# Forgetting attention two heads at a time on halves of TensorE's array, and joint gates in the mixer

## Chip, cores and metric

One core of a Trainium2 chip runs the whole program. The metric is the device time of one execution in microseconds: three runs of the kernel before gave 2260.94 to 2266.46, median 2263.86.

## The reference, cut

A token mixer with a 16-expert layer (272 positions: 16 learned tokens and 256 inputs, width 1024) is followed by two layers of a second block (256 positions, width 1024). The change touches two places: the gates of the first mixer and the forgetting attention of the second block's first layer.

```python
def _token_mixer(h, norm_g, w_in, b_gates, ...):
    proj = jnp.einsum('bnd,dk->bnk', _rmsnorm(h, norm_g), w_in)
    rq, rk, rv, rg, mq, mk, mv, mo, gate_pre = jnp.split(proj, SPLIT_AT, axis=-1)
    ...
    gts = gate_pre.astype(f32) + b_gates.astype(f32)          # 16 columns
    log_i = gts[..., :8]                                      # 2 directions x 4 heads
    log_f = jax.nn.log_sigmoid(gts[..., 8:])
    ...
def forgetting_attention(q, k, v, log_f):                     # 8 heads of 64, 256 positions
    cum = jnp.cumsum(log_f, axis=1).transpose(0, 2, 1)
    for blk in range(seq // 128):
        lo, hi = blk * 128, (blk + 1) * 128
        s = einsum("bqhd,bkhd->bhqk", q[:, lo:hi], k[:, :hi]) * scale      # scale = 1/8
        s = s + cum[:, :, lo:hi, None] - cum[:, :, None, :hi]
        s = jnp.where(causal, s, NEG_INF)
        outs.append(einsum("bhqk,bkhd->bqhd", softmax(s), v[:, :hi]))
def fox_shortconv_mixer(h, w_in, b_f, conv_w, w_out):
    q, k, v, f_logit, b_gate, c_gate, u = jnp.split(h @ w_in, ...)
    log_f = jax.nn.log_sigmoid(f_logit + b_f)
    y_b = b_gate * causal_depthwise_conv(c_gate * u, conv_w)
    return concatenate([forgetting_attention(...), y_b]) @ w_out
```

In words: the first mixer holds retention and mLSTM heads and a convolution; each of 16 experts takes the 34 positions that score highest and computes a gated layer of 2816 hidden columns; the second block's layers have this mixer or a recurrent one, attention to a memory, and a gated feed-forward layer.

## The kernel before, in words

The program is written by hand, one instruction stream for each engine, with semaphores between them; no planner sets an order. By time it has these stages: the first mixer (0 to 224 us), the experts (224 to 1537), the junction to the second block (to about 1584), the forgetting attention with the rest of its layer's input projection (1583.67 to 1663.84), and the remainder, which is output projection, memory attention, feed-forward, and the second layer (to 2261).

**Weights.** Dense weights come in chunks of 256 columns by DMA from SP's queue into a ring of slots. ScalarE rounds a chunk to the narrower float type that the dense products take (the high part, L2047, in the first mixer L1673), VectorE subtracts it from the float original (the low part, L2734, in the first mixer L2352). TensorE then makes three products for each tile of 128 rows, high by high, low by high and high by low (`three_passes`, L1296; in the first mixer L788 and L806). The slots that the experts stream through are those of the mixer, so their transfers start as the mixer lets go.

**Start.** POOL fills a constant tile `ones` (L679). TensorE's first work is the transposes of the tokens (L751, L763), which wait for VectorE's copy; then `project_first` and `project_tile` (L777 to L809) run through the projection. The gates (L829 to L838) are two groups of 24 products, one with the eight input-gate columns as stationary operand into bank 4 and one with the eight forget-gate columns into bank 5, each streaming 272 positions. VectorE adds the two biases (L2423 to L2428).

**Attention, TensorE.** The eight heads lie two in a tile of 128 features, head n in rows 64 (n mod 2) and up of tile n/2.
- `fox_scores(n)` (L1401): block 0 (L1405) and block 1 (L1406) into bank 5, on 64 rows of the array; and a product that lays head n's cumulative row out over all 128 partitions, into bank 6 (L1407), its stationary operand a table `pick` of 8 rows.
- `fox_transposes(n)` (L1410): waits for exponentials n and until transposes n-1 have been copied out; turns three blocks of 128 (L1418) into bank 7. Its wait is for `att_probs`, which VectorE raises when head n's exponentials are scaled.
- `fox_values(n)` (L1421): waits for the copy of the transposes; two products with 64 stationary columns (L1429, L1430) into half of bank 4.
- The main loop (L1434 to L1471) puts between them one half chunk (24 products) of the input projection at a time: scores n+1, half, transposes n, half, values n.

**Attention, VectorE** (L2880 to L2961). `fox_args(n)` builds the part that isn't the product: causal bar minus cumulative row (L2889, two blocks), minus the cumulative row (L2890), then scores by 1/8 plus that (L2891), and two maxima (L2895, L2896). `att_normalise(n)` takes reciprocals (L2901) and scales the two blocks (L2903). The loop over n runs normalise(n), args(n+1), then for some n the low parts of the outputs or a quarter of the short convolution (L2915 to L2927), then `split_weights_to(10 + n)`, one low part.

**Attention, ScalarE** (L2111 to L2148). `fox_softmax(n)`: two exponentials with sums (L2030). `take_fox_probs(n)`: the transposes out of bank 7 (L2125). The loop runs softmax(n+1), take probs(n), one weight cast, and for some n the copy of a finished projection.

The cumulative row itself is made before the loop by VectorE (L2870 to L2877) from eight logit rows, by a scan. SP loads the causal bar and the table (L658 to L661).

## Time and profile before

| | value |
|---|---|
| three runs | 2260.94 to 2266.46 us, median 2263.86 |
| profiled execution | 2263.05 us, its span 2261.2, mean granted clock 0.99 |
| PE busy | 2144.1 us, 95%, 12021 instructions |
| PEld busy | 1295.1 us, 57% |
| DVE busy | 719.3 us, 32%, 1034 instructions |
| ACT busy | 643.7 us, 28%, 1024 instructions |
| POOL busy | 40.2 us, 2% |
| moved by DMA | 724.65 MB, 320 GB/s over the span |

PE is TensorE's products, PEld its loading of stationary operands (beside the products), DVE VectorE, ACT ScalarE. The span runs from the first to the last instruction of the trace; the execution's own time is 1.85 us longer. Rows of the timeline give start, duration, engine, line, operation, destination<-sources, shapes and how many alike follow each other; in square brackets stands the idle time of that engine ahead of the row and what ended it.

### The profile page before, as it was taken

The page shows a single profiled execution, that of the slowest core. Times are in us where ns is not written, and L with a number is a line of the kernel's source. Part 1 is how long each engine was busy: PE and PEld are TensorE (multiplying, and loading weights), DVE is VectorE, ACT ScalarE, POOL GpSimd, SP SyncE. Part 2 cuts the span into 40 slices and gives each one's busy share as a digit, 9 for nine tenths or more (in the row PEclk, how much of TensorE's full clock was granted, in tenths as well). Part 3 has the DMA queues.
Part 4 walks back from the last instruction along what each step waited for, and adds up shares of the span by engine and source line. Part 5 has one row for each costly group of instructions (what it writes and reads, how often), then busy time and mean ns, then how long its engine had stood idle before and what let it go on. Part 6 is the DMA issues. An engine that isn't in the chain of part 4 may idle for free.

```text
span 2261.2 us, 27131 instructions
## 1 busy us (share of the span) xinstructions
PE 2144.1 (95%) x12021; PEld 1295.1 (57%) x12021; DVE 719.3 (32%) x1034; ACT 643.7 (28%) x1024; POOL 40.2 (2%) x70
## 2 busy tenths in 40 slices
PE   8999999998998998999998998999999999999999
PEld 7877443333333333333333333337888998988997
DVE  7775100110110110110110010016665654875553
ACT  6555110100100110110110010005465444865442
POOL 3111000000000000000000000000000000000000
PEclk9999999999999999999999999999999999999999
DMA  7436999999999999999999999997444655554553
GB/s 233 145 108 277 408 406 430 430 425 429 429 425 430 429 426 430 430 425 429 429 425 430 429 421 430 429 427 230 130 167 132 218 191 187 185 168 149 196 187 112
DMA packets 152879, 724.65 MB, mean 320 GB/s; under 512 B 8606, under 2 KB 106322, under 8 KB 127546
## 3 DMA queue, kind: packets, MB, share of 16 engines
q1 hardware_dynamic: 151544, 720.85, 79.9%
q8 instruction: 95, 1.56, 0.3%
q0 software_dynamic: 640, 1.43, 0.2%
q10 hardware_dynamic: 578, 0.64, 0.1%
q14 instruction: 22, 0.18, 0.0%
HBM read 721.82 MB, written 1.07 MB: 320 GB/s over the span
## 4 chain that ended last, share of the span: by engine, by line
PE 63%; DMA 31%; ACT 3%; DVE 2%; issue 1%; SPq 0%; ACTq 0%; DVEq 0%
PE bank L1296 22%; PE bank L1176 17%; DMA weight_ring<-in_w_down_dram 15%; DMA weight_ring<-in_w_up_dram 11%; PE bank L1143 5%; PE bank L1254 5%; DMA weight_ring<-in_w_gate_dram 4%; PE bank L806 4%; PE bank L1325 1%; PE bank L1009 1%; PE bank L1490 1%; PE bank L1513 1%; ACT weights_ring L2047 1%; PE bank L1279 1%; DVE weights_ring L2734 0%
## 5 line engine op out<-in xcount | busy, mean ns | idle before, releaser
L1176 PE MATMUL bank<-weight_ring,arena 128*64 128x506 f32 x3048 | 647.0, 563 | 24.4 <-DMA weight_ring<-in_w_up_dram 16.7
L1176 PEld LDWEIGHTS bank<-weight_ring,arena 128*64 128x64 f32 x3048 | 213.5, 134 | 416.6 <-issue 377.7
L1254 PE MATMUL bank<-weight_ring,arena 128*64 128x512 f32 x1408 | 336.2, 631 | 62.3 <-DMA weight_ring<-in_w_down_dram 62.3
L2702 DVE SCALAR_TENSOR_TENSOR arena<-arena,bank 128x506 f32<-128x506 f32 (+1 forms) x48 | 28.0, 639 | 915.6 <-ACT arena L1946 915.6
L2734 DVE TENSOR_TENSOR weights_ring<-weight_ring,weights_ring 128x2048 fp32r<-128x2048 f32 x110 | 249.7, 2289 | 145.0 <-ACT weights_ring L2047 144.8
L1254 PEld LDWEIGHTS bank<-weight_ring,arena 128*64 128x64 f32 x1408 | 103.3, 144 | 284.2 <-issue 202.1
L1296 PE MATMUL bank<-input_high,weights_ring 128*128 128x256 f32 x1920 | 245.7, 280 | 0.0
L1296 PEld LDWEIGHTS bank<-input_high,weights_ring 128*128 128x128 f32 x1920 | 232.0, 188 | 2.6 <-issue 2.3
L2047 ACT ACTIVATE weights_ring<-weight_ring 128x2048 fp32r<-128x2048 f32 x109 | 205.6, 1908 | 61.3 <-DMA weight_ring<-in_w_ffn_down_dram 41.3
L1143 PE MATMUL bank<-arena 128*128 128x256 f32 x512 | 142.9, 404 | 0.0
L1143 PEld LDWEIGHTS bank<-arena 128*128 128x128 f32 x512 | 87.3, 189 | 82.6 <-issue 75.6
L1296 PE MATMUL bank<-input_low,weights_ring 128*128 128x256 f32 x960 | 131.0, 278 | 0.0
L1938 ACT ACTIVATE arena<-bank 128x512 f32<-128x512 f32 x16 | 9.6, 597 | 415.5 <-PE bank L1143 415.5
L1296 PEld LDWEIGHTS bank<-input_low,weights_ring 128*128 128x128 f32 x960 | 120.1, 188 | 0.0
L1966 ACT ACTIVATE squares<-bank 128x512 f32<-128x512 f32 x16 | 9.6, 597 | 388.3 <-PE bank L1254 388.3
L1914 ACT ACTIVATE squares<-bank 128x512 f32<-128x512 f32 x15 | 9.0, 597 | 333.3 <-PE bank L1114 333.3
L1296 PE MATMUL bank<-weights_ring,mixed_high 128*128 128x512 f32 x320 | 94.8, 400 | 1.5 <-DVE weights_ring L2734 1.5
L2695 DVE TENSOR_TENSOR hT<-hT,bank 128x512 f32<-128x512 f32 x60 | 38.6, 684 | 164.7 <-PE bank L1195 164.7
L1296 PE MATMUL bank<-weights_ring,hidden_high_a 128*128 128x512 f32 x256 | 70.4, 395 | 0.0
L1296 PEld LDWEIGHTS bank<-weights_ring,mixed_high 128*128 128x128 f32 x320 | 59.1, 188 | 15.3 <-issue 2.5
L806 PE MATMUL bank<-mixer_high_a,weights_ring 128*128 128x272 f32 x420 | 64.5, 296 | 0.0
L1296 PE MATMUL bank<-weights_ring,mixed_low 128*128 128x512 f32 x192 | 60.2, 395 | 0.0
(402 smaller groups left out, 1975.7 us busy)
## 6 DMA issues: line engine op xcount, KB each, us to landing
weight_ring<-in_w_up_dram SPq DMA_DIRECT2D x63, 2816.0 KB, 19.9
weight_ring<-in_w_down_dram SPq DMA_DIRECT2D x63, 2816.0 KB, 21.8
weight_ring<-in_w_gate_dram SPq DMA_DIRECT2D x60, 2816.0 KB, 18.9
weight_ring<-in_w_ffn_gu_dram SPq DMA_DIRECT2D x44, 1024.0 KB, 5.1
weight_ring<-in_w_ffn_down_dram SPq DMA_DIRECT2D x22, 1024.0 KB, 4.9
weight_ring<-in_w_in_dram SPq DMA_DIRECT2D x16, 1024.0 KB, 5.9
arena<-in_w_xkv_dram SPq DMA_DIRECT2D x8, 2048.0 KB, 23.3
weight_ring<-in_ab_w_in_dram SPq DMA_DIRECT2D x12, 1024.0 KB, 5.9
```

Source lines behind the costliest of these rows:

```text
L806: last = pe.matmul(bank[pj.entries[A_FIRST[n]][0]][:, 0:T], (high, low, high)[part][:, i, c], mix_low[:, T * i:T * i + T] if part == 2 els ...
L1009: last = pe.matmul(bank[pj.entries[A_OUT[n]][0]][:, 0:T], (high, low, high)[part][:, i, c], mix_low[:, T * i:T * i + T] if part == 2 else ...
L1143: last = pe.matmul(bank[7][:, 256 * a:256 * a + 256], w, x, start=(i == 0 and a == 0), stop=(i == KT - 1), skip_group_check=True)
L1176: last = pe.matmul(bank[first_bank + c][MPAD * half:MPAD * half + MPAD, 0:(hi - lo) * HF], xs3[:, s, :], w[:, lo:hi, HF * half:HF * half + ...
L1254: last = pe.matmul(bank[6][MPAD * half:MPAD * half + MPAD, :], hidT[:, at:at + MPAD], W[:, j * D + 512 * half:j * D + 512 * half + 512], s ...
L1279: last = pe.transpose(feature_bank(j, t, half)[:, P * i:P * i + P], YG[:, at:at + P], ident[:])
L1296: last = pe.matmul(dst, w, y, start=start and n == 0, stop=stop and n == len(todo) - 1, skip_group_check=check)
L1325: last = pe.matmul(dst[:, 256 * t:256 * t + 256], x[:, i, tok], w[:, i, :], start=(n == 0 and i == 0), stop=(n == 2 and i == KT - 1))
L2047: act.activation(high_slot(k), raw_slot(k), ACT.Copy).then_inc(S("weights_high"), 1)
L2695: dve.tensor_tensor(rows, rows, bank[6 + n % 2][:], ALU.add).then_inc(S("scatter_taken"), 1)
L2702: dve.scalar_tensor_tensor(out=v, in0=v, scalar=1.0, in1=bank[c][:, 0:HF * (hi - lo)], op0=ALU.add, op1=ALU.mult)\
L2734: dve.tensor_tensor(low_slot(k), raw_slot(k), high_slot(k), ALU.subtract).then_inc(S("weights_low"), 1)
```

## The change

1. **Start.** TensorE makes 24 products of `ones` with itself into a bank nobody reads, waits for the tokens, makes 10 more, and only then turns the tokens. VectorE fills `ones` instead of POOL.
2. **Gates.** One group of 24 products with all 16 columns into bank 4. VectorE adds all 16 biases at once; behind the second of the following projection tiles one product with a piece of the identity brings rows 8 to 15 down to partitions 0 to 7 in bank 5, from where VectorE copies them.
3. **Scores.** `fox_scores(pair)` makes both heads of a tile, one on rows 0 to 63 of the array into bank 5, the other on rows 64 to 127 into bank 6. The cumulative rows come as a third product added in the same banks: high and low parts of the eight rows lie at partitions 0 and 32 (again at 64 and 96) of `fox_rows`, and one rounded product of 40 rows and 384 columns with a table of -8 adds them to the scores of each head.
4. **Arguments.** VectorE's part for one head is then one operation (scores by 1/8 plus a bar of three blocks) and the two maxima.
5. **Values.** `fox_values(pair)` makes both heads at once, one in columns 0 to 63 of the array, the other in 64 to 127.
6. **Order.** On TensorE two groups of transposes now stand one half chunk apart, behind them the pair's values and the next pair's scores. ScalarE and VectorE keep their loops, with the last steps arranged anew: the cast and the low part in step 6 are no longer left out, and the third quarter of the convolution is made in step 7.

The diff, cut to what the sentences speak of; the loop over 8 heads is ScalarE's, `fox_rows` is filled by VectorE ahead of its own loop:

```diff
+            pe.wait_ge(S("ones_ready"), 1)
+            for n in range(24):
+                pe.matmul(bank[7][:, 0:P], ones[:], ones[:], start=True, stop=True)
+            pe.wait_ge(S("tokens_landed"), 32)
+            for n in range(10):
+                pe.matmul(bank[7][:, 0:P], ones[:], ones[:], start=True, stop=True)
...
-            for g in range(2):
-                for part in range(3):
-                    for i in range(KT):
-                        last = pe.matmul(bank[4 + g][0:8, 0:T], (gh, gl, gh)[part][:, i, 8 * g:8 * g + 8],
...
+            for part in range(3):
+                for i in range(KT):
+                    last = pe.matmul(bank[4][0:16, 0:T], (gh, gl, gh)[part][:, i, :],
...
             for n in range(4):
                 project_tile(12 + n)
+                if n == 1:
+                    pe.wait_ge(S("gates_taken"), 1)
+                    pe.matmul(bank[5][0:8, 0:T], ident[0:16, 8:16], li[0:16], start=True, stop=True).then_inc(S("gates_ready"), 1)
...
+            def fox_scores(pair):
+                if pair:
+                    pe.wait_ge(S("att_scores_taken"), 2 * pair)
+                heads = [(bank[5 + n], slice(64 * n, 64 * n + 64)) for n in range(2)]
+                for dst, r in heads:
+                    pe.matmul(dst[:, 0:P], q3[r, pair, 0:P], k3[r, pair, 0:P], start=True, stop=False, skip_group_check=True)
+                for dst, r in heads:
+                    pe.matmul(dst[:, P:3 * P], q3[r, pair, P:2 * P], k3[r, pair, :], start=False, stop=False, skip_group_check=True)
+                for n, (dst, r) in enumerate(heads):
+                    rows = slice(64 * n, 64 * n + 40)
+                    at = P * (2 * pair + n)
+                    pe.matmul(dst[:, 0:3 * P], fox_pick[rows, at:at + P], fox_rows[rows, :], start=False, stop=True,
+                              skip_group_check=True).then_inc(S("att_scores"), 1)
+            def fox_values(pair):
+                pe.wait_ge(S("pt_taken"), 2 * pair + 2)
+                if pair:
+                    pe.wait_ge(S("mixed_low"), pair)
...
+            ab_half(3, 0)
...
+            fox_scores(0)
+            ab_half(3, 1)
+            ab_half(6, 0)
+            fox_scores(1)
+            ab_half(6, 1)
+            fox_transposes(0)
+            ab_half(8, 0)
+            fox_transposes(1)
+            ab_half(8, 1)
+            fox_values(0)
+            pe.wait_ge(S("proj_taken_act"), taken_after("act", C["ab", 3]))
+            fox_scores(2)
+            ab_half(10, 0)
+            fox_transposes(2)
+            ab_half(10, 1)
+            fox_transposes(3)
+            ab_half(7, 0)
+            fox_values(1)
+            fox_scores(3)
+            ab_half(7, 1)
+            fox_transposes(4)
+            ab_half(9, 0)
+            fox_transposes(5)
+            ab_half(9, 1)
+            fox_values(2)
+            ab_half(11, 0)
+            fox_transposes(6)
+            ab_half(11, 1)
+            fox_transposes(7)
...
+            out_pair(("ab_out", 2), 1, 0, mixed(2), first=True)
+            fox_values(3)
...
             for n in range(8):
-                if n < 6:
+                if n < 7:
                     fox_softmax(n + 1)
-                    take_fox_probs(n)
-                elif n == 6:
-                    take_fox_probs(6)
-                    fox_softmax(7)
-                else:
+                take_fox_probs(n)
+                if n == 7:
                     conv_high(2)
-                    take_fox_probs(7)
                 cast_weights_to(10 + n)
...
+            dve.tensor_copy(fox_rows[0:8, P:3 * P], frow[0:8])
+            after(dve.tensor_copy(fox_rows[0:8, 0:P], frow[0:8, 0:P]))
+            dve.tensor_tensor(fox_rows[32:40, P:3 * P], frow[0:8], fox_rows[0:8, P:3 * P], ALU.subtract)
+            after(dve.tensor_tensor(fox_rows[32:40, 0:P], frow[0:8, 0:P], fox_rows[0:8, 0:P], ALU.subtract))
+            dve.tensor_copy(fox_rows[64:104], fox_rows[0:40]).then_inc(S("fox_row_ready"), 1)
...
-                dve.tensor_tensor(nm3[:, 0:3:2, :], bar2, cum, ALU.subtract)
-                after(dve.tensor_scalar(nm3[:, 1, :], bank[6][:, 0:P], -1.0, None, ALU.mult))
-                dve.scalar_tensor_tensor(out=e, in0=bank[5][:, 0:384], scalar=0.125, in1=fox_nm, op0=ALU.mult, op1=ALU.add)\
+                dve.scalar_tensor_tensor(out=e, in0=bank[5 + n % 2][:, 0:384], scalar=0.125, in1=fox_bar, op0=ALU.mult, op1=ALU.add)\
...
-                if n == 6:
+                if n == 7:
                     short_convolution(2)
-                elif n == 7:
                     conv_low(2)
-                if n != 6:
-                    split_weights_to(10 + n if n < 7 else 16)
+                split_weights_to(min(10 + n, 16))
```

**How it moves instructions.** TensorE before, around heads 0 and 1 (L1405 to L1407 scores and cumulative row, L1296 half a chunk in two rows, L1418 transposes, L1429 and L1430 values):

```order
L1405 MATMUL bank<-arena 128x128
L1406 MATMUL bank<-arena 128x256
L1407 MATMUL bank<-arena 128x256
L1296 MATMUL bank<-input_high,weights_ring 128x256 x16
L1296 MATMUL bank<-input_low,weights_ring 128x256 x8
L1418 MATMUL bank<-ident,squares 128x128 x3
L1296 MATMUL bank<-input_high,weights_ring 128x256 x16
L1296 MATMUL bank<-input_low,weights_ring 128x256 x8
L1429 MATMUL bank<-squares,arena 64x256
L1430 MATMUL bank<-squares,arena 64x128
L1405 MATMUL bank<-arena 128x128
```

The same place after the change (L1310 half a chunk, L1439 transposes, L1449 and L1451 values, L1422, L1424 and L1428 scores with the cumulative rows):

```order
L1439 MATMUL bank<-ident,squares 128x128 x3
L1310 MATMUL bank<-input_high,weights_ring 128x256 x16
L1310 MATMUL bank<-input_low,weights_ring 128x256 x8
L1439 MATMUL bank<-ident,squares 128x128 x3
L1310 MATMUL bank<-input_high,weights_ring 128x256 x16
L1310 MATMUL bank<-input_low,weights_ring 128x256 x8
L1449 MATMUL bank<-squares,arena 64x256 x2
L1451 MATMUL bank<-squares,arena 64x128 x2
L1422 MATMUL bank<-arena 128x128 x2
L1424 MATMUL bank<-arena 128x256 x2
L1428 MATMUL bank<-fox_rows,fox_pick_high 128x384 x2
```

Between two groups of transposes stood two halves, values and scores; now one half stands between the two of a pair, and values and the next scores follow each other directly.

VectorE before, from one head's argument to the next head's scaling (L2889 to L2896 argument and maxima, L2734 the low part of a chunk, L2901 and L2903 the scaling):

```order
L2889 TENSOR_TENSOR arena<-arena,bank 128x2x128
L2890 TENSOR_SCALAR arena<-bank 128x128
L2891 SCALAR_TENSOR_TENSOR squares<-bank,arena 128x384
L2895 TENSOR_REDUCE small<-squares 128x1
L2896 TENSOR_REDUCE small<-squares 128x1
L2734 TENSOR_TENSOR weights_ring<-weight_ring,weights_ring 128x2048
L2901 RECIPROCAL small<-small 128x2
L2903 TENSOR_SCALAR squares<-squares,small 128x128
L2903 TENSOR_SCALAR squares<-squares,small 128x256
```

and after the change:

```order
L2927 SCALAR_TENSOR_TENSOR squares<-bank,squares 128x384
L2931 TENSOR_REDUCE small<-squares 128x1
L2932 TENSOR_REDUCE small<-squares 128x1
L2768 TENSOR_TENSOR weights_ring<-weight_ring,weights_ring 128x2048
L2937 RECIPROCAL small<-small 128x2
L2939 TENSOR_SCALAR squares<-squares,small 128x128
L2939 TENSOR_SCALAR squares<-squares,small 128x256
```

Two operations of the argument are gone; the low part of a chunk stands where it stood, ahead of the next head's scaling.

## Rows read from the trace of the kernel before

**Rows 1.** Busy by stretch: us, PE PEld DVE ACT POOL (count), clock, DMA, GB/s.

```profile
24.41:54.68 30.27, 30.27 (x243) 30.23 (x241) 29.28 (x40) 22.17 (x35) 8.49 (x10) 1.00 0.66 195
54.68:60.63 5.95, 5.95 (x51) 4.25 (x48) 5.81 (x8) 1.23 (x4) 1.17 (x2) 1.00 0.61 179
224.16:1537.18 1313.02, 1223.85 (x5723) 469.61 (x5723) 115.60 (x233) 125.62 (x210) 0.85 (x2) 0.98 1.00 425
1583.67:1663.84 80.17, 80.17 (x508) 66.52 (x507) 51.79 (x101) 37.80 (x74) 0.00 (x0) 1.00 0.39 126
```

**Rows 2.** Timeline of TensorE over one head of the attention.

```profile
1604.17 0.65 PE L1429 MATMUL bank<-squares,arena 128*64 128x256 f32 x2
...
1604.96 0.48 PE L1405 MATMUL bank<-arena 64*128 64x128 f32 x2
1605.29 0.59 PE L1406 MATMUL bank<-arena 64*128 64x256 f32 x2
1605.81 0.69 PE L1407 MATMUL bank<-arena 8*128 8x256 f32 x2
1606.43 2.15 PE L1296 MATMUL bank<-input_high,weights_ring 128*128 128x256 f32 x16
...
1609.37 0.49 PE L1418 MATMUL bank<-ident,squares 128*128 128x128 f32 x3
...
1612.62 0.65 PE L1429 MATMUL bank<-squares,arena 128*64 128x256 f32 x2
```

**Rows 3.** Timeline of ScalarE beside the same head.

```profile
1608.63 0.40 ACT L2030 ACTIVATE squares<-squares,small 128x128 f32<-128x128 f32 x1 [3.18 <-DVE small L2896]
...
1610.28 1.91 ACT L2047 ACTIVATE weights_ring<-weight_ring 128x2048 fp32r<-128x2048 f32 x1
```

**Rows 4.** Timeline of VectorE ahead of the attention and beside that head.

```profile
1576.78 2.29 DVE L2734 TENSOR_TENSOR weights_ring<-weight_ring,weights_ring 128x2048 fp32r<-128x2048 f32 x1 [2.17 <-ACT weights_ring L2047]
...
1612.22 2.29 DVE L2734 TENSOR_TENSOR weights_ring<-weight_ring,weights_ring 128x2048 fp32r<-128x2048 f32 x1 [3.29 <-ACT weights_ring L2047]
1614.43 0.16 DVE L2901 RECIPROCAL small<-small 128x2 f32<-128x2 f32 x1
...
1615.09 0.41 DVE L2889 TENSOR_TENSOR arena<-arena,bank 128x256 f32<-128x256 f32 x1
...
1615.74 0.56 DVE L2891 SCALAR_TENSOR_TENSOR squares<-bank,arena 128x384 f32<-128x384 f32 x1
...
1616.86 0.68 DVE L2915 TENSOR_TENSOR hT<-bank,hT 128x512 f32<-128x512 f32 x1
...
1620.68 2.29 DVE L2734 TENSOR_TENSOR weights_ring<-weight_ring,weights_ring 128x2048 fp32r<-128x2048 f32 x1
```

**Rows 5.** Timeline of TensorE at the start, and one row of the junction.

```profile
10.08 2.37 PE L751 MATMUL bank<-ident,arena 128*128 128x128 f32 x10 [10.08 <-DVE arena L2364]
...
16.88 1.95 PE L788 MATMUL bank<-mixer_high_a,weights_ring 128*128 128x272 f32 x7
...
18.86 1.57 PE L788 MATMUL bank<-mixer_high_a,weights_ring 128*128 128x272 f32 x7
...
20.39 1.05 PE L788 MATMUL bank<-mixer_high_a,weights_ring 128*128 128x272 f32 x7
...
1539.10 4.29 PE L1269 MATMUL bank<-ident 128*128 128x128 f32 x36
```

**Rows 6.** Timeline of VectorE in the first mixer.

```profile
24.10 0.42 DVE L2410 TENSOR_SCALAR arena<-arena,vec_cols 128x272 f32<-128x272 f32 x1 [0.75 <-ACT arena L1740]
...
39.98 2.28 DVE L2352 TENSOR_TENSOR weights_ring<-weight_ring,weights_ring 128x2048 fp32r<-128x2048 f32 x1
```

**Rows 7.** Costliest groups of instructions: busy, mean ns, idle before and its releaser.

```profile
L1176 PE MATMUL bank<-weight_ring,arena 128*64 128x506 f32 x3048 | 647.0, 563 | 24.4 <-DMA weight_ring<-in_w_up_dram 16.7
```

**Rows 8.** TensorE's timeline at a late expert transfer, and the 5 us around it.

```profile
449.41 7.07 PE L1254 MATMUL bank<-weight_ring,arena 128*64 128x512 f32 x24 [2.19 <-DMA weight_ring<-in_w_down_dram]
...
450.00:455.00 5.00, 5.00 (x18) 1.44 (x16) 0.00 (x0) 0.00 (x0) 0.00 (x0) 0.66 1.01 433
```

105 lines of the change are left out of this document (41 added, 64 removed).

## Prediction, made before the changed kernel was run

> **What bounds the kernel now.** I read the program as stages first (busy time in stretches), because one share for the whole span hides four different limits [rows 1]. The profiled execution took 2263.05 us, 0.81 less than the median of the runs shown, and all sums below are made against 2263.05. In the mixer TensorE is busy for all of 24.41 to 60.63, while the transfers use 0.61 to 0.66 of their time. From 224.16 to 1537.18 the DMA share is 1.00 at 425 GB/s: that stage starts when the mixer lets go of its slots and then lasts as long as its bytes do, so what the mixer gains or loses arrives whole at 1537. From 1583.67 to 1663.84, the forgetting attention, TensorE is busy in 80.17 of 80.17 us, VectorE in 51.79, ScalarE in 37.80. A full TensorE is no proof that TensorE alone sets the pace, though: the timeline of one head on the three engines tells how much slack the other two have [rows 2 to 4], and that is what the change uses up.
>
> **Edit 1, dummy products at the start.** The clock row says 1.00 from time 0, but durations tell more: ten transposes of 128 columns take 2.37 us, 0.237 each, while 36 passes of the same size take 4.29 late in the program, 0.119 each: full against half rate [rows 5]. Of the 48 products of the first tile, eight starts take 1.53 us from 18.86, the next eight 1.02 us from 20.39, so the rise was at about 20.0, roughly 3.1 us after TensorE had begun to run without gaps at 16.88; the 2.8 dense microseconds from 10.08 did not do it. The new 24 products start at about 1.1 us (the memset of ones moves to VectorE, which is idle there) and are 48 passes, the 10 behind the tokens 20 more. With a rise after the same 3.1 us: 13 slow passes to 4.2, 35 fast ones to 8.4, 20 more to 10.8. The transposes then begin 0.7 us late but last 1.2 instead of 2.37, and are done 0.5 earlier. Everything behind them on TensorE runs at full rate, up to 3 us ahead at 24.41. It can't keep that: VectorE is busy in 29.28 of the next 30.27 us. Its convolutions begin at 24.10 after a gap of 0.75 which is all that row offers (I allow 1.2 with the small gaps before it), and its subtraction for the fifth chunk ends at 42.26 [rows 6], where TensorE arrives at 24.41 plus six tiles of 3.03 (ten in 30.27), 42.6: slack 0.3. So the front gives 1.05 to 1.6, **I take 1.3**. The other end: a rise only 9.9 us after the first product (as from 10.08 to 20.0 before) makes 42 slow passes and lets the dummies end at 14.1. The transposes end 3.0 us late, VectorE starts so much later, and after the slack 2.7 us are lost. The shorter wait is the nearer row, since the new products leave no gap.
>
> **Edit 2, joint gates.** 48 products in 5.95 us [rows 1] become 24, since eight or sixteen stationary columns stream the same 272: minus 2.98. One 272-column product with the identity is added, two passes; by the passes of 128 columns at 0.119 [rows 5] it costs 0.5. Its wait for VectorE's sum is covered by the second tile projected after the gates. **Net 2.5 saved.** One constant load less on POOL's queue is worth nothing: nobody waits for it.
>
> **Edit 3, the attention's own work.** Per head the scores take 0.33, 0.52 and 0.62 us, 1.47 in all, the values 0.79, the three transposes 0.25 [rows 2]; between them lie halves of projections of 2.94 to 3.0 us. Eight heads: 11.8 for scores, 6.3 for values. Now four groups each. For the values both halves of the columns are used at once; the expert products do this, 3048 passes of 506 columns in 647.0 us, 0.212 each [rows 7], where one in flight would take 0.47 by the passes in rows 5. So a pair costs what a head did, 0.85 (upper bound 1.5). For scores on two halves of the rows no row exists: if they run together a pair is 0.33 + 0.52, plus the single-pass product of 384 columns, 0.35 to 0.45: 1.3. If one follows the other, 2.1. I take 1.3, nearest to the column halves. TensorE's own work shrinks by 18.1 minus 8.6, with fewer changes of kind about **9.9 us** (3.8 if nothing runs together).
> The Trainium skill (TensorEngine Tiling (Array Packing), Key Properties) says that tiles load and multiply independently, and that a change of tiling mode drains the array. No run here shows row halves; by the page the pair would be at my lower price.
>
> **What the new order exposes.** Each transposition starts a chain. Its scores are copied out and ScalarE begins the next weight cast 0.91 us after it; the cast lasts 1.93 to VectorE's subtraction, that 2.21, and behind it, in program order, stands the scaling of the next head, 0.66 with a hand-over of 0.1 [rows 3, 4]. Together 5.8 us from one head's transposes to the earliest of the next. Before, 8.45 us of TensorE's work lay between them, and the chain was hidden with 2.6 us to spare. Now pairs stand one half apart: 0.25 + 2.97 = 3.2 us. **TensorE waits 2.6 us** before transposes 1, 3 and 5: 7.8 in all.
> The next pair's scores wait until both accumulators of the last pair are read. From transposes 1: the argument and its maxima 1.1, exponentials 1.0, copy 0.4, cast 1.9, subtraction 2.2, scaling 0.66, argument 0.6: 7.8 us, less what overlaps at the start. TensorE has one half, the transposes and the values, 4.1: **3.8 us** wait before pair 2. Before pair 3 the short convolution stands on VectorE too, 3.82 us [rows 4], longer than the copy and cast beside it: 8.3 against 4.1, **4.2 us**. Before transposes 6, 7.3 against 7.0: 0.3. Before transposes 7 the argument and exponentials of head 7 come first, 7.3 against 3.2: **4.1**. Sum 20.3 us of waits. VectorE's two removed operations (0.65 per head between its rows at 1615.09 and 1615.74) are already taken out of these chains. The six new operations before the first score stand where VectorE next waits 2.17 us for a cast, at 1576.78 [rows 4]; the POOL cast and the larger tables have twenty microseconds. They cost nothing.
> Net for the attention: 20.3 minus 9.9, **10.4 us slower**.
>
> **The clock in the new waits.** In the expert stage TensorE waits 2.09 us or more seventeen times, the first at 449.41; after ten of them the granted clock falls to 0.50 for about three microseconds (0.66 over the five behind the first) [rows 8], after seven it does not. So some of six waits of 2.6 to 4.2 us will run at half rate behind them, 1.7 us each. Behind transposes 1 and 3 that is swallowed by the next wait; behind the scores of pairs 2 and 3, transposes 5 and transposes 7 it is not: at two chances in three, and now and then a longer low, **4.7 us** (none 0, all 7).
>
> **Sum.** 2263.05 - 1.3 - 2.5 + 10.4 + 4.7 = 2274.3.
>
> **Rivals.**
> (a) The weight work does not stand in the chain. It decides below one length: if transposes to transposes were under 3.2 us, TensorE would not wait, and the change would give its 9.9 and 3.8: 2249.4. For it speaks that TensorE is the only full engine; against it the rows of ScalarE and VectorE, where cast, subtraction and scaling follow each other without a gap, in an order that the change keeps.
> (b) Row halves and column halves do not run together: 3.8 saved in place of 9.9, with two of the waits shorter by 0.7 and 0.65: attention plus 14.3, and 2277 to 2279. Against it the column halves of the experts.
> (c) The dummies come too slowly: 4.0 worse at the front, 2278.3. For it speaks that the dense 2.8 us at 10.08 raised nothing.
> (d) Waits about half as long, because ScalarE reaches casts earlier than I think: 5 us less and no fall, about 2262 to 2265. Nothing in the rows speaks for it.
> The skill's TensorEngine Tiling (Array Packing), PSUM Bottleneck, warns that tiling speeds TensorE but not what is read out of PSUM. The trace agrees, with VectorE at 51.79 us of 80.17 but each head's read-out queued behind 2.21 us of weight work.
>
> **How the numbers follow.** Forecast 0.62, (a) 0.07, (b) 0.12, (c) 0.11, (d) 0.08. The predicted time is the forecast's, 2274. Its own ends are 2270 (clock never falls) and 2278. The range leaves out (a) and the lowest part of (d), and takes in the upper ends of (b) and (c): 2265 to 2282. Faster or slower is told apart from no change at 0.2%, 4.5 us, about what a measurement of this kernel can tell: faster 0.08 ((a) and a little), same 0.09 (most of (d)), slower 0.83.
>
> **What would show it.** TensorE's row for the attention should fall from full to about three quarters busy, with idle gaps of 2.6 us before every second group of transposes, ended by VectorE's scaling, and about 4 us before the scores of pairs 2 and 3, ended by VectorE's argument. VectorE's scaling should still follow its weight subtraction directly. The gates should take 3.0 us, the first dense product of the projections should start near 22, and the expert stage should start 3.8 us earlier. I am wrong if TensorE has no gap before transposes 1, if the gaps are there but the stage is not longer, or if the experts start later than before.

## The result, and the profile after

The changed kernel takes 2270.07 us (median of seven runs, 2268.16 to 2276.87) beside 2263.32 for the one before (seven runs, 2259.57 to 2267.50): ratio 1.0031, 95% interval 1.0021 to 1.0041. It is slower by 6.8 us. The forecast was 2274, with 2265 to 2282 as its range. The profiled span grew from 2261.2 to 2268.3 us, by 7.1.

Where the difference lies, read from TensorE's timeline at the same places of both programs (us from the span's start, and what each stage adds):

| place on TensorE | before | after | shift | the stage adds |
|---|---|---|---|---|
| first tile of the projection done | 24.41 | 21.89 | -2.52 | |
| gates begin | 54.68 | 53.61 | -1.07 | |
| gates done | 60.63 | 56.62 | -4.01 | -2.94 |
| experts begin | 224.16 | 220.40 | -3.76 | +0.25 |
| experts done | 1537.18 | 1535.23 | -1.95 | +1.81 |
| first scores | 1583.67 | 1581.73 | -1.94 | 0 |
| transposes of the junction behind | 1663.84 | 1675.05 | +11.21 | +13.15 |
| last down projection begins | 2194.25 | 2201.28 | +7.03 | -4.18 |

The stretches of the profile after that answer to [rows 1] (length, busy time and count of TensorE's products, its weight loads, VectorE, ScalarE, POOL, granted clock, DMA share, GB/s):

```profile
21.89:53.61 31.72, 30.73 (x243) 30.35 (x241) 30.22 (x50) 22.98 (x38) 9.18 (x10) 1.00 0.71 212
53.61:56.62 3.01, 3.01 (x27) 2.32 (x25) 2.90 (x5) 0.80 (x3) 1.23 (x2) 1.00 0.47 103
220.40:1535.23 1314.83, 1226.25 (x5723) 470.23 (x5723) 115.59 (x233) 125.61 (x210) 0.84 (x2) 0.98 1.00 425
1581.73:1675.05 93.32, 74.52 (x500) 65.15 (x499) 46.75 (x85) 36.73 (x74) 0.00 (x0) 0.95 0.34 112
```

In the last row TensorE was busy for 80.17 of 80.17 us before. It now has 5.7 us less to do and the stage lasts 13.2 longer: 18.8 us of gaps have appeared where there were none, and the granted clock is no longer 1.00. VectorE's busy time fell too, 51.79 to 46.75. No engine is full any more.

TensorE's timeline shows the gaps (start, duration, engine, line, operation; in brackets the idle time ahead and what ended it). L1439 are transposes, L1422 to L1428 scores, L1449 values:

```profile
1581.73 0.49 PE L1422 MATMUL bank<-arena 64*128 64x128 f32 x4
1582.05 0.60 PE L1424 MATMUL bank<-arena 64*128 64x256 f32 x4
1582.30 0.53 PE L1428 MATMUL bank<-fox_rows,fox_pick_high 40*128 40x384 f32 x2
1582.76 2.15 PE L1310 MATMUL bank<-input_high,weights_ring 128*128 128x256 f32 x16
...
1592.64 0.49 PE L1439 MATMUL bank<-ident,squares 128*128 128x128 f32 x3
1592.88 2.06 PE L1310 MATMUL bank<-input_high,weights_ring 128*128 128x256 f32 x16
...
1598.50 0.55 PE L1439 MATMUL bank<-ident,squares 128*128 128x128 f32 x3 [2.65 <-DVE squares L2939]
...
1606.35 0.49 PE L1422 MATMUL bank<-arena 64*128 64x128 f32 x4 [3.67 <-DVE squares L2927]
...
1607.38 3.66 PE L1310 MATMUL bank<-input_high,weights_ring 128*128 128x256 f32 x16
...
1617.68 0.90 PE L1439 MATMUL bank<-ident,squares 128*128 128x128 f32 x3 [2.54 <-DVE squares L2939]
1618.23 3.37 PE L1310 MATMUL bank<-input_high,weights_ring 128*128 128x256 f32 x16
...
1625.93 0.49 PE L1422 MATMUL bank<-arena 64*128 64x128 f32 x4 [2.59 <-DVE squares L2927]
...
1635.76 0.55 PE L1439 MATMUL bank<-ident,squares 128*128 128x128 f32 x3 [2.54 <-DVE squares L2939]
...
1650.35 0.55 PE L1439 MATMUL bank<-ident,squares 128*128 128x128 f32 x3 [3.92 <-DVE squares L2939]
```

Six waits: 2.65, 2.54, 2.54 and 3.92 us at transposes 1, 3, 5 and 7, ended by VectorE's scaling (L2939); 3.67 and 2.59 at the scores of pairs 2 and 3, ended by VectorE's argument (L2927). The rows at 1607.38 and 1618.23 are half chunks at half rate: 3.66 and 3.37 us where 2.15 is usual.

The chain between transposes 0 at 1592.64 and transposes 1 at 1598.50, first on ScalarE (L2161 the copy, L2083 the weight cast), then on VectorE (L2768 the low part, L2937 and L2939 the scaling of head 1), where it answers to [rows 3, 4]:

```profile
1593.16 0.49 ACT L2161 ACTIVATE squares<-bank 128x384 f32<-128x384 f32 x1 [2.88 <-PE bank L1439]
1593.55 1.91 ACT L2083 ACTIVATE weights_ring<-weight_ring 128x2048 fp32r<-128x2048 f32 x1
```

```profile
1595.49 2.29 DVE L2768 TENSOR_TENSOR weights_ring<-weight_ring,weights_ring 128x2048 fp32r<-128x2048 f32 x1 [6.23 <-ACT weights_ring L2083]
1597.70 0.16 DVE L2937 RECIPROCAL small<-small 128x2 f32<-128x2 f32 x1
1597.89 0.55 DVE L2939 TENSOR_SCALAR squares<-squares,small 128x128 f32<-128x128 f32 x2
```

Note the brackets: ScalarE had idled 2.88 us and VectorE 6.23 us before this. Neither lacks time. Head 1's exponentials were done at 1590.3; its scaling stood behind a low part that waited for a cast that waited, in program order only, for head 0's transposes.

The start, answering to [rows 5]. The first row of dummies is 48 passes in 8.0 us, and the transposes are then at full rate:

```profile
1.12 8.17 PE L756 MATMUL bank<-ones 128*128 128x128 f32 x48 [1.12 <-DVE ones L2374]
9.12 2.40 PE L759 MATMUL bank<-ones 128*128 128x128 f32 x20
11.36 1.25 PE L763 MATMUL bank<-ident,arena 128*128 128x128 f32 x10
...
15.59 1.14 PE L800 MATMUL bank<-mixer_high_a,weights_ring 128*128 128x272 f32 x7
```

### The profile page after: what moved, and what is told of

It reads as the page before. It is cut to its first block, busy times and chain, and to the rows that moved or that the text cites. A ratio compares the mean times of both kernels' runs of the same rounds, so it can differ in the third digit from the quotient of the medians.

```text
span 2268.3 us, 27197 instructions
## 1 busy us (share of the span) xinstructions
PE 2141.3 (94%) x12059; PEld 1295.9 (57%) x12059; DVE 715.4 (32%) x1025; ACT 642.0 (28%) x1024; POOL 43.8 (2%) x69
## 3 DMA queue, kind: packets, MB, share of 16 engines
HBM read 722.44 MB, written 1.07 MB: 319 GB/s over the span
## 4 chain that ended last, share of the span: by engine, by line
PE 60%; DMA 31%; ACT 4%; DVE 4%; issue 1%; DVEq 0%; SPq 0%; ACTq 0%
PE bank L1310 20%; PE bank L1190 17%; DMA weight_ring<-in_w_down_dram 15%; DMA weight_ring<-in_w_up_dram 11%; PE bank L1157 5%; PE bank L1268 5%; DMA weight_ring<-in_w_gate_dram 4%; PE bank L818 4%; DVE weights_ring L2768 1%; PE bank L1339 1%; ACT weights_ring L2083 1%; PE bank L1023 1%; ACT squares L2012 1%; PE bank L1526 1%; PE bank L1549 1%
## 5 line engine op out<-in xcount | busy, mean ns | idle before, releaser
L2768 DVE TENSOR_TENSOR weights_ring<-weight_ring,weights_ring 128x2048 fp32r<-128x2048 f32 x110 | 249.7, 2289 | 154.9 <-ACT weights_ring L2083 154.8
L1310 PE MATMUL bank<-input_high,weights_ring 128*128 128x256 f32 x1920 | 245.5, 281 | 0.0
L1310 PEld LDWEIGHTS bank<-input_high,weights_ring 128*128 128x128 f32 x1920 | 232.2, 190 | 1.8 <-issue 1.5
L2083 ACT ACTIVATE weights_ring<-weight_ring 128x2048 fp32r<-128x2048 f32 x109 | 205.6, 1908 | 66.8 <-DMA weight_ring<-in_w_ffn_down_dram 41.1
L1310 PE MATMUL bank<-input_low,weights_ring 128*128 128x256 f32 x960 | 129.6, 277 | 0.0
L1310 PEld LDWEIGHTS bank<-input_low,weights_ring 128*128 128x128 f32 x960 | 118.9, 188 | 0.0
L1310 PE MATMUL bank<-weights_ring,mixed_high 128*128 128x512 f32 x320 | 95.1, 403 | 1.5 <-DVE weights_ring L2768 1.5
L1310 PE MATMUL bank<-weights_ring,hidden_high_a 128*128 128x512 f32 x256 | 70.4, 395 | 0.0
L1310 PEld LDWEIGHTS bank<-weights_ring,mixed_high 128*128 128x128 f32 x320 | 60.0, 190 | 15.2 <-issue 2.0
L1310 PE MATMUL bank<-weights_ring,mixed_low 128*128 128x512 f32 x192 | 60.7, 397 | 0.0
```

The costliest lines, as they stand in the source:

```text
L1310: last = pe.matmul(dst, w, y, start=start and n == 0, stop=stop and n == len(todo) - 1, skip_group_check=check)
L2083: act.activation(high_slot(k), raw_slot(k), ACT.Copy).then_inc(S("weights_high"), 1)
L2768: dve.tensor_tensor(low_slot(k), raw_slot(k), high_slot(k), ALU.subtract).then_inc(S("weights_low"), 1)
```

## The experiments

The runs of this section come from three chips. The kernel before ran beside them each time, at medians of 2267.96 to 2268.47 us instead of 2263.32, so that ratios and not times are to be compared with the result. Two theories stood at first. **The chain**: weight work that stands, by program order, between one head's transposes and the next head's scaling makes TensorE wait. **The pairs**: products on halves of the array, or reading out two banks, are themselves what holds the stage up. For each kernel the table at the end of this section gives the attention stage from the first scores to the junction's transposes, since a whole run moves by some microseconds between executions.

**The change taken apart.** The first kernel has only the new start, the second only the joint gates, the third only the attention (each is the part of the diff that its name says).

> The kernel before with the dummy products at the start alone (and ones filled by VectorE). In the changed kernel's trace the first dense product starts 2.5 us earlier and the gates 1.07 us earlier, so theory A (the rest is lost to a full VectorE, what is left is carried through the experts whole) expects the experts to start 1.0 to 1.1 us earlier and the time to fall by as much: ratio 0.9995, 2262.2 beside a before of 2263.3. Theory B (the experts last as long as they do because of something else, and take a gain at their front away) expects the experts to end where they did: ratio 1.0000.

> The kernel before with joint gates alone. Theory A: gates 3.0 instead of 5.95 us, minus the 0.3 to 0.5 of the product that brings rows down, all of it on TensorE's path: the experts start 2.6 to 2.7 us earlier and end as much earlier, ratio 0.9988. Theory B: the experts start 2.6 us earlier and end within 1 us of before, ratio 0.9997 to 1.0000.

> The kernel before with the attention's part of the change alone (pairs, single-pass cumulative rows, new order). If the attention is what made the kernel slower: the stretch from the first scores to the transposes of the junction behind it is 13 us longer than before, with the same six waits (2.6, 3.7, 2.5, 2.6, 2.5, 3.9 us), and the whole 3.8 us more above before than the full change: plus 10.5 to 13, ratio 1.0046 to 1.0058. If instead the 4.1 us by which the second layer's feed-forward ran faster in the changed kernel's profile belong to this part, the total is plus 9 to 11; if they are chance between executions, plus 13.

Measured: start alone 0.9991 (0.9978 to 1.0004), gates alone 0.9986 (0.9976 to 0.9997), attention alone 1.0062 (1.0045 to 1.0080). The product of the three is 1.0039, inside the interval of the whole change. The slowdown is the attention's: 93.42 us for the stage with the same six waits as in the full change (2.54, 3.68, 2.54, 2.60, 2.65 and 3.92); its ratio is a little above the 1.0046 to 1.0058 expected, which the interval still reaches. For the start the clock times can't tell theory A from B (the interval holds both); the gates' interval excludes 1.0000 and holds A's 0.9988, but does not exclude B's 0.9997.

Where the experts begin, both small kernels missed what was expected of them. With the start alone the gates begin at 53.52 instead of 54.68, as forecast, but the experts begin at 224.39, 0.23 us later than before. With the gates alone the experts begin at 223.16, 1.00 us earlier where 2.6 to 2.7 were expected. Up to the last twelve products ahead of the experts' own both gains are there: these begin at 218.76 and 217.41, against 219.93 before. Then the granted clock falls in the two small kernels and not in the kernel before (stretch of these products; before, start alone, gates alone):

```profile
219.93:223.20 3.27, 2.80 (x12) 0.89 (x13) 0.27 (x2) 1.65 (x5) 2.72 (x3) 1.00 0.99 417
```

```profile
218.76:223.43 4.67, 4.20 (x12) 1.15 (x13) 0.27 (x2) 1.63 (x5) 4.06 (x4) 0.63 1.01 425
```

```profile
217.41:222.20 4.79, 4.32 (x12) 1.15 (x13) 0.27 (x2) 1.63 (x5) 4.18 (x4) 0.64 1.01 426
```

Eight of the eleven profiles of this study have that fall, at a price of 1.4 to 1.7 us. The kernel before, the first profile of the change and the one with the gaps filled don't. The experts themselves last 1315.42 and 1314.73 us in the two small kernels, beside 1314.94 before: no sign that they take a gain at their front away, as theory B has it.

**The loops arranged by pairs.** TensorE's order is untouched. The diff is cut: VectorE's loop first, behind the dots ScalarE's.

```diff
-            for n in range(8):
-                att_normalise(n, ...)
-                if n < 7:
-                    fox_args(n + 1)
...
-                split_weights_to(min(10 + n, 16))
+            for pair in range(4):
+                fox_args(2 * pair)
+                fox_args(2 * pair + 1)
+                for n in (2 * pair, 2 * pair + 1):
+                    att_normalise(n, ...)
+                if pair:
+                    fox_low(pair - 1)
+                split_weights_to((11, 12, 14, 16)[pair])
+                if pair == 1:
+                    short_convolution(0)
...
+            for pair in range(4):
+                fox_softmax(2 * pair)
+                fox_softmax(2 * pair + 1)
...
+                cast_weights_to((10, 12, 14, 16)[pair])
+                take_fox_probs(2 * pair)
...
+                if pair < 3:
+                    cast_weights_to((11, 13, 15)[pair])
+                take_fox_probs(2 * pair + 1)
...
```

> The changed kernel with ScalarE's and VectorE's loops arranged by pairs: arguments, exponentials and scaling of both heads first, then the two casts and the two low parts, so that no weight work stands between one head's transposes and the other's scaling. TensorE's order is that of the changed kernel. The theory that the weight work in the chain makes the waits expects the waits at transposes 1, 3, 5, 7 and at the scores of pair 2 to vanish and one of about 1.5 us at the scores of pair 3 to stay, no fall of the clock, and so 18 to 20 us less than the changed kernel: 2250 to 2252, ratio to before 0.994 to 0.995. The rival that pairs are held up by something else (products on halves of the array that don't overlap, read-out of the banks, the order on TensorE itself) expects waits of the same sum in other places and 2266 to 2272.

Measured: 2257.68 us beside 2268.21, ratio 0.9951 (0.9933 to 0.9970), stage 72.44 us, clock 1.00. On TensorE there is no gap at any second transposes any more; a short one of 0.18 at the scores of pair 2, and two remain (L1422 scores of pair 3, where about 1.5 us was expected, and L1449 values of pair 2, where none was):

```profile
1594.08 0.49 PE L1439 MATMUL bank<-ident,squares 128*128 128x128 f32 x3
...
1597.13 0.49 PE L1439 MATMUL bank<-ident,squares 128*128 128x128 f32 x3
...
1614.25 0.49 PE L1422 MATMUL bank<-arena 64*128 64x128 f32 x4 [1.78 <-DVE squares L2934]
...
1625.78 0.65 PE L1449 MATMUL bank<-squares,arena 128*64 128x256 f32 x4 [1.10 <-ACT squares L2161]
```

Same products on the same halves of the array, same number of read-outs, 21 us less in this stage than with the changed kernel's loops: the theory of the pairs falls. The ratio is just above the 0.994 to 0.995 expected.

**One link cut, then the other.** Two small edits of the changed kernel, each of which moves one step by one place in one loop.

```diff
                 if n < 7:
                     fox_softmax(n + 1)
+                if n < 7:
+                    cast_weights_to(10 + n)
                 take_fox_probs(n)
                 if n == 7:
                     conv_high(2)
-                cast_weights_to(10 + n)
+                    cast_weights_to(10 + n)
```

> The changed kernel with one line moved: in each step ScalarE makes its weight cast before it copies the transposes, not after, so the cast no longer waits for transposes and the chain is cut at one link. The theory of the chain expects no wait at transposes 1, 3 and 5, waits of about 2.2 and 3.2 us at the scores of pairs 2 and 3 and of 2.4 us at transposes 7 (the low part still stands ahead of the next scaling), and a stretch of 81 to 83 us for the attention instead of 93.3: 10 to 12 us less than the changed kernel, ratio to before 0.998 to 0.999. The rival that the pairs themselves are held up expects the stretch unchanged within 1 us.

```diff
+            att_normalise(0, ...)
             for n in range(8):
-                att_normalise(n, ...)
                 if n < 7:
                     fox_args(n + 1)
+                    att_normalise(n + 1, ...)
...
                 split_weights_to(min(10 + n, 16))
```

> The changed kernel with VectorE's scaling of the next head moved from behind the low part to ahead of it (directly behind its argument); ScalarE's loop unchanged. It cuts the chain at the other link. The theory expects the waits at transposes 1, 3, 5 and 7 to go, since the scaling no longer waits for cast and low part; but ScalarE still casts behind each copy of the transposes, so the copy of the second head of a pair comes late (a wait of about 1.1 us at the values) and the next pair's arguments are still queued behind two low parts: 3.8 us at the scores of pair 2 as before, and about 6 at those of pair 3, where the short convolution now also stands. Sum 13 instead of 18 us, with falls of the clock behind the two long waits: stretch 86 to 90 us instead of 92.3 to 93.3. If the waits had nothing to do with the place of the low part, the stretch is unchanged within 1 us.

Measured, cast ahead: stage 84.10, a little above the 81 to 83 expected, ratio 0.9990 (0.9980 to 1.0000). The waits at transposes 1, 3 and 5 are gone, the three others are 2.30, 3.89 and 2.48 (2.2, 3.2 and 2.4 expected), with half-rate stretches behind both scores. Two short ones that were not expected have come at the values, 0.43 and 1.14 us, for ScalarE's copy. Scaling ahead: stage 87.47, ratio 1.0017 (1.0001 to 1.0032), and this timeline:

```profile
1601.01 0.65 PE L1449 MATMUL bank<-squares,arena 128*64 128x256 f32 x4 [1.33 <-ACT squares L2161]
...
1605.70 0.80 PE L1422 MATMUL bank<-arena 64*128 64x128 f32 x4 [3.81 <-DVE squares L2927]
...
1619.15 0.65 PE L1449 MATMUL bank<-squares,arena 128*64 128x256 f32 x4 [1.33 <-ACT squares L2161]
...
1626.04 0.80 PE L1422 MATMUL bank<-arena 64*128 64x128 f32 x4 [6.02 <-DVE squares L2927]
```

No wait at transposes, 1.33 three times at the values, 3.81 and 6.02 at the scores (1.1, 3.8 and about 6 expected). A wait that a chain makes does not vanish when one link is cut. It moves to the next thing that the remaining links hold up, and how far can be worked out from the same durations (3.89 us at the scores of pair 3, against 3.2 expected, is the worst miss of the two kernels).

**The gaps filled.** Does the idle gap make the clock fall, and what does the fall cost? `fill(count, chunk, half)` makes `count` products of `ones` with itself, in a bank that only TensorE writes at that time; two of the six places are shown.

```diff
+            fill(8, 8, 1)
             fox_transposes(1)
...
+            fill(12, 10, 0)
             pe.wait_ge(S("proj_taken_act"), taken_after("act", C["ab", 3]))
             fox_scores(2)
```

> The changed kernel with dummy products of 128 columns (8, 12, 8, 12, 8 and 13 of them, 1.9 to 3.1 us) just ahead of the six waits, in banks that only TensorE writes then, so that TensorE works through most of each wait. If the idle gaps make the clock fall, no half chunk runs at half rate any more: 1.5 us less behind the scores of pair 2 and 1.7 us behind transposes 7; the one behind transposes 3 was swallowed by the next wait, whose gap grows back from 2.6 to about 4.1. Together 3.2 us less than the changed kernel, a stretch of 90 us. If the fall has another cause than the gap, the slow halves stay and the stretch stays at 93.3.

```profile
1601.82 2.94 PE L1460 MATMUL bank<-ones 128*128 128x128 f32 x24
1605.57 0.49 PE L1422 MATMUL bank<-arena 64*128 64x128 f32 x4 [0.81 <-DVE squares L2941]
...
1606.60 2.15 PE L1310 MATMUL bank<-input_high,weights_ring 128*128 128x256 f32 x16
...
1619.50 2.94 PE L1460 MATMUL bank<-ones 128*128 128x128 f32 x24
1623.64 0.49 PE L1422 MATMUL bank<-arena 64*128 64x128 f32 x4 [1.20 <-DVE squares L2941]
```

No half chunk is slow any more, the granted clock is 1.00 over the stage, and the stage is 90.69 us: 2.6 less than in the first profile of the change and 1.6 less than in the second (below). The wait at the scores of pair 3 has grown back as expected: 2.94 us of dummies and 1.20 of gap, 4.14 in all. The runs agree: six took 2274.82 to 2276.76 us, five of the changed kernel on the same chip 2278.21 to 2280.30 (ratios to before 1.0030, interval 1.0018 to 1.0041, and 1.0044), medians 3.3 us apart where 3.2 was expected. How much of that is the attention stage's is less sure, since the profiles put 1.6 to 2.6 us there. Gaps of 0.76 to 1.20 us were left, and none was followed by a fall in this execution. That a short gap never is does not follow: the falls just ahead of the experts came behind waits of 0.99, 0.43 and 0.90 us within 3 us.

**Two waits more removed**, by three moves in the version by pairs: the first short convolution one pair later, the low parts one chunk later, and a cast behind the copy of head 5 instead of ahead of it. The diff is cut to these:

```diff
-                if pair == 1:
+                if pair == 2:
                     short_convolution(0)
...
-                split_weights_to((11, 12, 14, 16)[pair])
+                split_weights_to((10, 12, 13, 16)[pair])
...
-                if pair < 3:
-                    cast_weights_to((11, 13, 15)[pair])
+                if pair < 2:
+                    cast_weights_to((11, 13)[pair])
                 take_fox_probs(2 * pair + 1)
+                if pair == 2:
+                    cast_weights_to(15)
```

> The version by pairs with three more moves: the first short convolution stands behind the arguments of pair 2 instead of ahead of them, the low parts follow their casts one pair later, and the probabilities of head 5 are copied before the cast that waits for its transfer. The version by pairs still waited 1.78 us at the scores of pair 3 and 1.10 us at the values of pair 2; if these two are the convolution and that cast, both go: stretch of the attention 69.4 instead of 72.4 us, 3 us less in all, ratio to before 0.9935 to 0.994. If the low parts that come later hold up a half chunk, the gain is less than 1 us.

Measured: 2251.77 us beside 2268.47, ratio 0.9925 (0.9911 to 0.9939), stage 70.01:

```profile
1582.47:1652.48 70.01, 68.66 (x499) 60.85 (x499) 47.07 (x85) 36.79 (x74) 0.00 (x0) 1.00 0.46 149
```

Both waits are gone and one of 0.44 us at transposes 7 has come, which waits for ScalarE's copy of head 6. The gain in the stage, 2.4 us, is a little under the 3 expected, while the ratio is below the 0.9935 to 0.994 expected; part of that is chance outside the stage (the last column of the table below). This is the fastest version of the study.

**The changed kernel once more**, for what is chance between executions.

> The changed kernel itself once more, beside these and beside before on the same chip: ratio 1.003 to 1.005. Its first profile differed from that of before by minus 3.8 us up to the experts, plus 1.8 in the experts, plus 13.2 in the attention and minus 4.3 between the attention and the last down projection. If the last figure is chance between executions, that stretch is within 1 us of before's or of the other runs' this time (521 to 525 us); if it belongs to the change, it is 517 again.

Measured: 2278.69 beside 2268.47, ratio 1.0044 (1.0031 to 1.0056). The stretch from the attention to the last down projection took 525.61 us, not 517.

| kernel | experts | attention stage | rest up to the last down projection |
|---|---|---|---|
| before | 1314.94 | 80.17 | 521.25 |
| changed, first profile | 1316.75 | 93.32 | 516.99 |
| changed, second | 1316.14 | 92.27 | 525.61 |
| start alone | 1315.42 | 80.17 | 525.14 |
| gates alone | 1314.73 | 79.82 | 525.21 |
| attention alone | 1316.45 | 93.42 | 525.37 |
| by pairs | 1316.41 | 72.44 | 524.77 |
| cast ahead | 1316.75 | 84.10 | 525.22 |
| scaling ahead | 1315.88 | 87.47 | 517.23 |
| gaps filled | 1315.92 | 90.69 | 525.16 |
| by pairs, second | 1315.98 | 70.01 | 521.28 |

("experts" here reaches to the first product of the junction; "rest" starts at the second group of the junction's transposes.) The last column has three levels, near 517, 521 and 525 us. They don't belong to the kernel: the changed one is on two of them. The last section shows what they are made of.

## Why the prediction was right

**The sum, term by term.** It said -1.3 and -2.5 for the mixer, -9.9 for TensorE's own work, +20.3 for waits, +4.7 for the clock: +11.2 against the profile of before. The trace gives the following.

- *Start, -1.3.* The gates begin 1.07 us earlier, although the first tile ended 2.52 earlier: VectorE, busy for 30.22 of 31.72 us, ate the rest, as the step on slack said. Its subtraction for the fifth chunk ends at 41.34, and TensorE, idle since 40.45, goes on at 41.44 (the row names no releaser; the two times do):

```profile
39.06 2.28 DVE L2385 TENSOR_TENSOR weights_ring<-weight_ring,weights_ring 128x2048 fp32r<-128x2048 f32 x1
```

```profile
41.44 1.11 PE L818 MATMUL bank<-mixer_high_a,weights_ring 128*128 128x272 f32 x7 [0.99 <-issue]
```

  Over all profiles the gates begin at 53.16 to 53.75 in the eight with the new start and at 54.68, 54.84 and 56.00 in the three without, so that the gain is real, but its size depends on the execution of before that it is held against. Two details were off. The large transposes end at 12.6; forecast was 0.5 us before the 12.45 of [rows 5], but the dummies ended at 11.4 and not 10.8. And by its own terms the range is 1.05 to 1.5 (1.2 plus 0.3), not to 1.6.
- *Joint gates, -2.5.* Minus 2.94, plus 0.55 for the two passes of the product with the identity (63.82 to 64.37), minus a wait of 0.24 for ScalarE that before has at 72.25: about 2.7. The two terms together arrive at the experts as -3.76 (3.8 forecast). That this agrees so well is in part luck: neither of the two profiles compared has the fall of the clock ahead of the experts. The second profile of the change has it, and its experts begin at 221.65, 2.51 us earlier than before's.
- *Carried whole through the experts.* Not shown. The experts lasted 1.8 us longer in the first profile. Over eleven profiles this stage spreads from 1314.73 to 1316.75; the seven profiles of kernels with both mixer edits are at 1315.88 or more, of the four others three are at 1315.42 or less, one at 1316.45. Up to 1 us of the mixer's gain may be lost there; chance would do as well.
- *TensorE's work, -9.9.* With the gaps filled the stage has 83.99 us of busy time, 122 dummy passes of 0.12 among them: 69.3 of its own, against 80.17. That is -10.9. The scores of a pair take 1.03 us (1581.73 to 1582.76) where I took 1.3, the values 0.8. Row halves do run together: the first products of both heads take 0.32 us (1581.73 to 1582.05), where those of one head took 0.33 [rows 2]. The upper prices, 2.1 and 1.5, are excluded, and rival (b) with them. The forecast's own prices add up to 18.1 minus 8.6, 9.5; the 0.4 more, for fewer changes of kind, had no row.
- *Waits, 20.3.* Forecast 2.6, 3.8, 2.6, 4.2, 2.6, 0.3 and 4.1. Measured 2.65, 3.67, 2.54, 2.59, 2.54, about 0.1 and 3.92, sum 18.0 (the forecast terms add up to 20.2, recorded as 20.3). The one that is off, at the scores of pair 3, is 4.14 when the clock doesn't fall ahead of it; so 19.5 in the forecast's terms. Another 0.8 us appeared that was not forecast: the junction's transposes at the end, at 1675.05, wait 0.80 for VectorE.
- *Clock, 4.7.* The work at half rate costs 74.52 minus 69.3, 5.2 us, of which 1.5 is swallowed by the wait behind it: 3.7. The mechanism, its size per fall (1.5 to 1.7 us) and the swallowing were right; which waits are followed by a fall differs between executions. In the first profile it was the scores of pair 2 and transposes 3 and 7, in the second transposes 1 and 5 and the scores of pair 3.
- Together -10.9 + 19.5 + 0.8 + 3.7 = 13.1, beside a measured 13.15; forecast 15.1.

**Why 2270 and not 2274.** Of the 4.1 us between the forecast difference (11.2) and that of the spans (7.1), 2.0 are the attention's mis-sized terms, 1.8 go the other way in the experts, and 4.2 come from a stretch that the change doesn't touch: layer 2 ran faster in the profile after. The second profile of the same kernel has none of that gain, and the ratio measured then, 1.0044, is 10.0 us.

**The rivals.** (a), that the weight work isn't in the chain, is what the two versions by pairs turn into fact. Its price, 2249.4, is 13.7 us less than before; the two versions take 10.5 and 16.7 us less than the before beside them. (b) falls by the 1.03 us; its sum doesn't come out either, since 20.3 less 3.8, 0.7 and 0.65 is 15.2 and not 14.3, which makes it 2279.1. (c), the dummies too slow: of 48 passes in 8.0 us (7.3 in the profile of the start alone), at 0.237 and 0.119 each, 19 (13) were slow, so half rate lasted 4.6 (3.1) us, between the two ends given; the dummies were over at 11.4, not 14.1. (d), waits half as long, falls by the waits.
The Trainium skill (TensorEngine Tiling (Array Packing), PSUM Bottleneck) says that tiling speeds TensorE but not what is read out of PSUM. In this trace it was not the read-out's speed that ran short: VectorE was busy for 46.75 of 93.32 us, and what was late was the read-out's place in the queue.

**What the argument rested on.** The row that decided was not a busy share. VectorE and ScalarE were under two thirds busy before [rows 1], and the waits followed from how far apart in TensorE's order two dependent steps stand (3.2 us, 8.45 before) beside how long the chain between them takes (5.8 us).

## What to carry to other kernels

When steps are regrouped on a full engine, compare for every pair of dependent steps the work that is left between them with the latency of the chain that joins them, and count in that chain everything that the other engines' program order puts ahead of its links. If the chain is longer, regroup the loops of the other engines in the same way as the first: here the same pairs cost 13 us with loops by head and gained 10 with loops by pair. Where two causes are near in price, judge an edit by its own stage in the trace; a total can hide 4 to 8 us of chance.

## What the runs showed of the hardware that was not expected

- **The clock can fall again right behind a warm-up.** In the first profile of the change the projection starts at full rate (7 starts in 1.14 us). In the profile of the start alone the transposes of 128 columns are at full rate as well, but behind the 14 small passes the first products of the projection are slow again (rows of the start alone, then the granted clock, last but two in the row, from 14 to 19 us: start alone 0.66, first profile of the change 1.00):

```profile
1.12 7.45 PE L748 MATMUL bank<-ones 128*128 128x128 f32 x48 [1.12 <-DVE ones L2346]
...
10.64 1.25 PE L755 MATMUL bank<-ident,arena 128*128 128x128 f32 x10
...
15.34 1.96 PE L792 MATMUL bank<-mixer_high_a,weights_ring 128*128 128x272 f32 x7
```

```profile
14.00:19.00 5.00, 5.00 (x24) 4.52 (x25) 5.00 (x9) 4.58 (x11) 4.65 (x9) 0.66 1.08 333
```

```profile
14.00:19.00 5.00, 5.00 (x34) 4.30 (x35) 4.97 (x8) 4.86 (x11) 4.16 (x8) 1.00 1.09 336
```

  The same holds in five of the other profiles with the dummies; of the eight only the first of the change and the one with the gaps filled, whose start is the same code, kept the rate. It costs little. Where the rate is kept, the first tile is done at 21.9 or 22.0, and TensorE then waits 0.99 us for VectorE's fifth low part; where it is lost, the tile is done at 22.6 to 23.2 and that wait is gone. The gates begin within 53.16 to 53.75 in all eight. Why the clock falls in one execution and not in another is open.
- **The same dense products run at more than one steady rate.** In the feed-forward of the second layer, granted clock 1.00 and TensorE fully busy in each, 10 us hold 87 products in the profile of before and in the second of the change, 90 or 91 in the first of the change, and 87 or 91 differ by 4 us over the stretch. The feed-forward of the first layer does the same, and independently, and the two together make the three levels of the table: both fast in the profiles near 517 us, the first fast and the second slow near 521, both slow near 525. In 60 us a fast one holds 531 or 532 products, a slow one 511 or 512, in each of the eleven profiles. No run here says why. In order: before, changed (first), changed (second), and then before again with 60 us of the first layer's and of the second's.

```profile
2100.00:2110.00 10.00, 10.00 (x87) 10.00 (x86) 5.08 (x6) 4.59 (x4) 0.00 (x0) 1.00 0.60 203
```

```profile
2110.00:2120.00 10.00, 10.00 (x90) 10.00 (x90) 5.50 (x6) 4.36 (x4) 0.00 (x0) 1.00 0.64 210
```

```profile
2120.00:2130.00 10.00, 10.00 (x87) 10.00 (x87) 5.69 (x4) 4.84 (x4) 0.00 (x0) 1.00 0.64 211
```

```profile
1773.00:1833.00 60.00, 60.00 (x532) 60.00 (x531) 35.52 (x29) 24.60 (x21) 0.00 (x0) 1.00 0.59 193
2113.00:2173.00 60.00, 60.00 (x512) 60.00 (x511) 32.60 (x26) 24.58 (x21) 0.00 (x0) 1.00 0.56 183
```
